# First block by token halves: output projection, queries and routing of tokens 0-127 ahead of the other half's attention

## The reference

```python
def first_block(...):
    ...
        h = rmsnorm(x, ln_mix_g[l]) * (1 + sc1) + sh1
        proj = h @ w_in[l]
        ...
        o_attn = nsa_mixer(q, kc, vc, ks, vs, kw, vw, gates, ...)
        o_conv = short_conv_mixer(ch, cb, cc, conv_w[l])
        mixed = jnp.concatenate([rmsnorm(o_attn, norm_attn_g[l]), rmsnorm(o_conv, norm_conv_g[l])], axis=-1)
        x = x + gt1 * (mixed @ w_out[l])

        h2 = rmsnorm(x, ln_ffn_g[l]) * (1 + sc2) + sh2
        x = x + gt2 * peer_ffn(h2, peer_wq[l], peer_keys[l], peer_u[l], peer_v[l])
    return rmsnorm(x, ln_final_g)
```

## Time and profile before

| | |
|---|---|
| median of 3 runs (lowest, highest) | 1507.47 us (1506.05, 1512.93) |
| profiled execution: its time, its span | 1513.2 us, 1511.3 us |
| mean granted TensorE clock | 0.948 of full |
| busy: PE, DVE, ACT, POOL | 1281.6 us (85%), 746.8 (49%), 477.1 (32%), 368.4 (24%) |
| gathers (q0 of the DMA queues) | 36864 packets, 268.45 MB, 43.3% of 16 engines' span |
| HBM read and written | 375.02 MB and 1.06 MB |

### The profile page before, as it was taken

How to read it: one execution, slowest core, us unless ns; L and a number is a source line. 1 busy time by engine, 2 the same in 40 slices (tenths; PEclk the granted TensorE clock), 3 DMA queues, 4 the chain that set the end, 5 groups by cost and what they waited for, 6 DMA issues and landing times.

```text
span 1511.3 us, 13142 instructions
## 1 busy us (share of the span) xinstructions
PE 1281.6 (85%) x4744; PEld 771.6 (51%) x4744; DVE 746.8 (49%) x1657; ACT 477.1 (32%) x1224; POOL 368.4 (24%) x285
## 2 busy tenths in 40 slices
PE   5899877887798887878889878699997789999896
PEld 1688545652233323223333322255775679999782
DVE  2313552748986696555544454511667764431212
ACT  1022220134343334344243333312785441111101
POOL 0688100134353454344334444100000000000000
PEclk9898888899999999999999999999998989999999
DMA  9775400599999999999999999645322130204130
GB/s 338 288 257 212 160 14 0 215 393 421 421 390 418 410 417 407 422 420 422 421 384 387 391 423 421 264 141 194 112 94 74 56 112 1 83 32 164 56 111 28
DMA packets 90827, 376.92 MB, mean 249 GB/s; under 512 B 6307, under 2 KB 8524, under 8 KB 57932
## 3 DMA queue, kind: packets, MB, share of 16 engines
q0 software_dynamic: 36864, 268.45, 43.3%
q1 hardware_dynamic: 52112, 103.46, 19.0%
q10 hardware_dynamic: 1788, 4.19, 0.9%
HBM read 375.02 MB, written 1.06 MB: 249 GB/s over the span
## 4 chain that ended last, share of the span: by engine, by line
PE 49%; DMA 21%; DVE 18%; ACT 8%; issue 2%; POOL 1%; SPq 0%; DVEq 0%; ACTq 0%; POOLq 0%
PE ps L87 49%; DMA AR<-in_puv,idx 19%; DVE AR L87 9%; DVE acc L87 3%; ACT L87 3%; DMA W<-in_w_mod 2%; ACT acc L87 2%; DVE tok L87 1%; ACT wv L87 1%; DVE RT L87 1%; ACT AR L87 1%; DVE hT L87 1%; ACT tok L87 1%; DVE junk L87 1%; POOL AR L87 1%
## 5 line engine op out<-in xcount | busy, mean ns | idle before, releaser
L87 PE MATMUL ps<-AR,acc 128*128 128x512 f32 x1024 | 500.5, 626 | 114.7 <-ACT acc L87 111.0
L87 DVE CUSTOM_DVE_ANT_0 AR<-AR,tok 128x1024 f32<-128x1024 f32 x256 | 312.6, 1223 | 219.0 <-DMA AR<-in_puv,idx 217.9
L87 POOL DMA_INDIRECT AR<-in_puv,idx x256 | 276.3, 1079 | 526.5 <-PE ps L87 390.3
L87 PEld LDWEIGHTS ps<-AR,acc 128*128 128x128 f32 x1024 | 183.8, 194 | 429.1 <-ACT acc L87 266.0
L87 PE MATMUL ps<-hT,W 128*128 128x256 f32 (+2 forms) x1504 | 323.1, 375 | 3.2 <-ACT hT L87 2.2
L87 PEld LDWEIGHTS ps<-hT,W 128*128 128x128 f32 (+1 forms) x1504 | 271.9, 198 | 46.1 <-issue 7.4
L87 ACT ACTIVATE wv<-av 128x1 f32<-128x1 f32 x256 | 51.5, 201 | 350.2 <-DVE av L87 349.9
L87 ACT ACT_TABLE_LOAD x90 | 115.5, 1283 | 16.8 <-issue 15.3
L87 ACT ACTIVATE acc<-K,wv 128x128 f32<-128x128 f32 x256 | 102.8, 402 | 8.4
L87 PE MATMUL ps<-W,hT 128*128 128x512 f32 (+3 forms) x288 | 95.2, 487 | 0.0
L87 ACT ACTIVATE wv<-wv,gw 128x1 f32<-128x1 f32 x256 | 75.4, 294 | 8.3
(11 more groups left out here) (199 smaller groups left out, 1035.8 us busy)
## 6 DMA issues: line engine op xcount, KB each, us to landing
W<-in_w_in SPq DMA_DIRECT2D x25, 2048.0 KB, 7.9
W<-in_w_mod SPq DMA_DIRECT2D x12, 2048.0 KB, 16.9
W<-in_w_out SPq DMA_DIRECT2D x2, 2048.0 KB, 10.3
W<-in_wq SPq DMA_DIRECT2D x2, 2048.0 KB, 10.3
AR<-in_puv,idx POOLq DMA_INDIRECT x256, 12.7
W<-in_wba SPq DMA_DIRECT2D x2, 2048.0 KB, 7.8
W<-in_wbb SPq DMA_DIRECT2D x2, 2048.0 KB, 7.7
W<-in_wo SPq DMA_DIRECT2D x2, 2048.0 KB, 7.8
```

The lines of the kernel that those rows point to most:

```text
L87: ins = f(*args, **kw)
```

## The change

The norms over the conv and attention channels, the convolution, the output projection's and the queries' functions take one half (and one weight tile) at a time. Emitted ahead of the gathers are half 0's parts, and of half 1's the units 4 and 5, `scores(6)` and the convolution. The rest of half 1 is a generator `half1`, which the loop over gathers advances by one piece per iteration from u = 1 on. The gathers begin with five slots (`ring`), since slots 5 and 6 lie over half 1's attention buffers in AR; these two are added when half 0's routing is done. `scores(u)` ends with the exponentials, and a new `weigh(u)` has its last three DVE operations, the normalisation. The routing has four batches of two heads (each pair of batches issues its `key_scores`), advanced by 2 DVE instructions per iteration below u = 32 and by 3 from there. Scratch moves: the keys into `R_LNF`, the routing's `sw` into `R_G2`, the scores of even units from 4 on into `R_POST`; so of the four broadcast rows only row 2 is loaded early and rows 1, 0 and 3 are loaded in the loop, and both halves of `mod_row` come together after half 1's routing. The diagonal matrices begin in the second half of `hT` and change to `acc[:, 0]` when `q_norm(1)` needs `hT`.

```diff
+        nrm = ar(4 * P).rearrange("p (n t) -> p n t", n=4)
+        junk = sb("junk", [P, D])
+        osq0 = junk[:, 0:512].rearrange("p (j t) -> p j t", j=4)
+        at[0] = 5 * 2 * D
...
-        for r in range(4):
-            SP.dma(nc.sync.dma_start, s_row, rowb[:, r, :], rows[r, :].partition_broadcast(P))
+        t_rows = {}
+
+        def load_row(r, after):
+            t_rows[r] = SP.dma(nc.sync.dma_start, s_rows[r], rowb[:, r, :], rows[r, :].partition_broadcast(P), after=after)
+
+        load_row(2, [])
...
+        def norm_root(key, n, src, after):
+            b = ps.take()
             for j in range(4):
-                t = V(stt, mixT[:, j, a * 128:a * 128 + 128], O[a].t[:, j * 128:j * 128 + 128], PV[:, V_NA + j:V_NA + j + 1],
-                      rat[:, a * 128:a * 128 + 128], MUL, MUL, after=[e, t_os[a]] + t_mc)
+                t = PE(mm, b.t[:, 0:P], ones, src[:, j, :], start=(j == 0), stop=(j == 3), after=b.old + after)
+            e = A(act, n, b.t[:, 0:P], ACT.Sqrt, scale=1.0 / 512, bias=eps, after=[t])
+            b.free = [e]
+            t_cn[key] = e
...
+        def attn_root(a):
+            t = A(act, osqs[a], O[a].t[:, :].rearrange("p (j t) -> p j t", j=4), ACT.Square,
+                  after=[stage[3 + 4 * a, "O"], stage[1 + 4 * a, "O"]] + t_g1 + t_c["o", 0] + t_c["o", 1])
+            t_os[a] = t
+            norm_root(("a", a), rats[a], osqs[a], [t])
+
+        def attn_mix(a):
+            e = V(rec, rats[a], rats[a], after=[t_cn["a", a]])
+            for j in range(4):
+                t = V(stt, mixT[:, j, a * P:a * P + P], O[a].t[:, j * P:j * P + P], PV[:, V_NA + j:V_NA + j + 1],
+                      rats[a], MUL, MUL, after=[e, t_os[a]] + t_mc)
+                t_mix[a].append(t)
             O[a].free = [t]
-            t_mix.append(t)
-        kT_sb = PT[:, 0, :]
+
+        t_oc, t_mix = [[], []], [[], []]
+        t_mc, t_g1 = [], []
+        kT_sb = R_LNF
         s_k = dsem("s_k")
-        t_keys = SP.dma(nc.sync.dma_start, s_k, kT_sb, keysT, after=[stage[7, "O"], stage[6, "O"]])
+        t_keys = SP.dma(nc.sync.dma_start, s_k, kT_sb, keysT)
...
-            for h0, nh in ((0, 2), (2, 2), (4, 4)):
-                bs, t = banks[h0 // 4]
+            for h0, nh in ((0, 2), (2, 2), (4, 2), (6, 2)):
+                if h0 % 4 == 0:
+                    bs, t = key_scores(a, h0 // 4)
...
-        ob1 = attn_mm(1)
-        routes = [route(0, kb, [stage[7, "O"]])]
+        qp = mixT
+        b2 = ps.take()
+        for n in range(4):
+            t_mc.append(mod_cols_sum(b2, 4 * n, *t_ms[n]))
+        sh2, sc2, t_m2 = mod_affine(b2, t_mc[3], 24, V_LNF, 16)
+        for n in range(2):
+            t_g1.append(mod_row_sum(2, n, *t_ms[4 + n]))
+        for j in range(4):
+            conv_step(j, 0)
+        turn_p(3)
+        pv_(2)
+        norm_root(("c", 0), nrm[:, 0, :], cbT[:, :, 0:P], t_oc[0])
+        pv_(3)
+        attn_root(0)
+        conv_mix(0)
+        scores(4)
+        attn_mix(0)
+        attn_mm(0, 0)
+        weigh(4)
+        for j in (0, 1):
+            conv_step(j, 1)
+        attn_mm(0, 1)
+        attn_add(0, 0)
+        turn_p(4)
+        scores(5)
+        attn_add(0, 1)
+        q_norm(0, [])
+        for j in (2, 3):
+            conv_step(j, 1)
+        weigh(5)
+        q_project(0, 0)
+        routes = [route(0, [])]
+        advance(routes[0], 1)
+        pv_(4)
+        turn_p(5)
+        norm_root(("c", 1), nrm[:, 1, :], cbT[:, :, P:2 * P], t_oc[1])
+        q_back(0)
+        q_project(0, 1)
+        scores(6)
         while (0, 0) not in t_idx or (0, 0) not in t_gw:
             advance(routes[0], 1)
-        attn_add(1, ob1)
-        queries(1)
-
+        pv_(5)
+        conv_mix(1)
+        ring = [[n, [t_gel[0], t_gel[1], t_cn["c", 1], t_mixfree[0]] + t_mix[1]] for n in range(5)]
+        late_t = {}
+
+        def half1():
+
+            weigh(6)
+            yield
+            turn_p(6)
+            load_row(1, [stage[6, "T"]])
+            yield
+            scores(7)
+            yield
+            pv_(6)
+            yield
+            weigh(7)
+            yield
+            turn_p(7)
+            yield
+            pv_(7)
+            yield
+            attn_root(1)
+            yield
+            attn_mix(1)
+            yield
+            attn_mm(1, 0)
+            yield
+            attn_mm(1, 1)
+            yield
+            attn_add(1, 0)
+            yield
+            attn_add(1, 1)
+            late_t["B"] = stage[7, "e"]
+            yield
+            late_t["dg"] = [t for f in dg_free for t in f]
+            q_norm(1, late_t["dg"])
+            yield
+            yield
+            q_project(1, 0)
+            yield
+            q_project(1, 1)
+            yield
+            q_back(1)
+            yield
...
-            slot_free[n] = [e]
+            ring.append([n, [e]])
             return e
 
         ahead = []
+        h1 = half1()
...
-            if routes:
-                advance(routes[0], 3)
-                if (0, 7) in t_gw and not second:
-                    second.append(1)
-                    routes = [route(1, [key_scores(1, 0), key_scores(1, 1)], [t_idx[0, 7], t_gw[0, 7]])]
-            if u in (64, 80):
-                t_g2.append(mod_row(3, (u - 64) // 16))
+            if u >= 1:
+                advance(h1, 1)
+            advance(routes[0], 2 if u < 32 else 3)
+            if (0, 7) in t_gw and len(routes) == 1 and len(t_h2[1]) == 2:
+                t_eq["hold"] = [late_t["B"]]
+                eqbuf[0] = acc[:, 1, :].rearrange("p (h s j) -> p h s j", h=4, s=16)
+                ring.append([5, [stage[7, "O"], t_mix[1][-1]]])
+                ring.append([6, [stage[7, "O"], t_mix[1][-1], t_eq["last"]]])
+                routes.insert(0, route(1, [t_idx[0, 7], t_gw[0, 7]]))
+            if (1, 7) in t_gw and len(routes) == 2:
+                routes.append(None)
+                load_row(0, [t_keyfree[-1]])
+                load_row(3, [t_idx[1, 7], t_gw[1, 7]])
+                for n in range(2):
+                    t_g2.append(mod_row(3, n))
```

More of the change, by code:

```diff
@@ L659, in build @@
-        t_mix = []
-        b = ps.take()
-        for j in range(4):
-            t = PE(mm, b.t[:, 0:S], ones, cbT[:, j, :], start=(j == 0), stop=(j == 3), after=b.old + [t_oc[j][1]])
-        rcv = z[:, 0, 0:S]
-        e = A(act, rcv, b.t[:, 0:S], ACT.Sqrt, scale=1.0 / 512, bias=eps, after=[t, t_oc[3][0]])
-        b.free = [e]
-        e = V(rec, rcv, rcv, after=[e])
-        for j in range(4):
-            t_mix.append(V(stt, mixT[:, 4 + j, :], oc[:, j, :], PV[:, V_NC + j:V_NC + j + 1], rcv, MUL, MUL, after=[e] + t_mc))
@@ L719, in queries @@
[L719 to L738 removed]
+        o_banks = {}
@@ new lines, in attn_mm, with attn_add @@
+        def attn_mm(a, n):
+            i, w, t_w = w_o[n]
+            b = ps.take()
+            t = token(w, 0, 512, mixT, a, t_w, t_mix[a], b, 0)
+            if a == 1:
+                done_w(i, t)
+            o_banks[a, n] = b, t
+            t_mixfree[a] = t
+        def attn_add(a, n):
+            b, t = o_banks[a, n]
+            o = junk[:, n * 512:n * 512 + 512]
+            xs = X[:, a, n * 512:n * 512 + 512]
+            e = V(tt_, o, b.t[:, :], R_G1[:, n * 512:n * 512 + 512], MUL, after=[t] + t_g1 + t_jx[-1:] + [t_cn["a", a]])
+            b.free = [e]
+            t_x1[a].append(V(tt_, xs, xs, o, ADD, after=[e]))
+            t_jx.append(t_x1[a][-1])
@@ new lines, in build, with q_norm, q_project @@
+        t_hx = {}
+        t_keyfree = []
+        def q_norm(a, free):
+            t_xb = norm_x(a, st[:, 12 + a:13 + a], t_x1[a], tok2, [stage[2 + 5 * a, "T"]])
+            t_hx[a], t_hx[a, "x"] = norm_T((a,), tok2, [t_xb], sc2, sh2, [t_m2] + free)
+        def q_project(a, n):
+            c = slice(a * 128, a * 128 + 128)
+            i, w, t_w = w_q[n]
+            b = ps.take()
+            for j in range(4):
+                for k in range(8):
+                    t = PE(mm, b.t[:, j * 128:j * 128 + 128], w[:, k, j * 128:j * 128 + 128], hT[:, k, c],
+                           start=(k == 0), stop=(k == 7), after=b.old + [t_w] + t_hx[a])
+            e = A(act, qp[:, 4 * n:4 * n + 4, c], b.t[:, :].rearrange("p (j t) -> p j t", j=4), ACT.Copy,
+                  after=[t, t_mixfree[a]])
+            b.free = [e]
+            t_qp[a].append(e)
+            if a == 1:
+                done_w(i, t)
@@ L1017, in build @@
                 rope("k", 0, t_rot["q", 0])
-        t_gfree = [f[0] for f in slot_free]
+        t_gfree = [f[0] for _, f in ring]
         t_pelast = e
```

179 lines of the change are left out of this document (68 added, 111 removed).

## The result

The changed kernel takes 1550.46 us (median of 4 runs, 1546.75 to 1558.36), the kernel before in the same session 1508.95 (4 runs, 1506.05 to 1512.93): ratio 1.028, 95% interval 1.0232 to 1.0328. It is slower by 41.5 us. The prediction had 1531 and a range to 1545: right in sign, too low in size, and the measured time lies above the range. The profiled execution has a span of 1549.8 us and a mean granted clock of 0.937 (before 1511.3 and 0.948).

What follows compares the result with a forecast made beforehand. The prediction took the DMA transfers of 256 expert-row gathers as the bound. Its terms, -9.3 + 3.7 + 24 + 3 - 1.5 + 3.7 = +23.6 us, moved the median from 1507.47 to 1531 us; range 1499 to 1545.

Steps and rivals of the forecast that it cites:

- First gather, 271: Start of the gathers: first gather at 271 us instead of 280.3, -9.3 us, bounds 263 and 278.
- scores(4) hold DVE to 194.0, the attention products end at 196.1: Steps ahead of the output projection: the attention root fits meanwhile, norm of the conv half ends at 189.7 us.
- The units, +24: Second half's pieces at units 1 to 19 among the gathers open transfer holes: +24 us, bounds 10 and 34.
- Only the lack of slots keeps them apart: Gathers with the second half: PE's 43 + 39 us of work against 85 us of transfers, separated by too few slots alone.
- +14: The units' idle if a gather takes 4.4 us by the Trainium skill, with an allowance of 3.5 us instead of 2.3.
- Five slots to unit 58, +3: Until head 7 is routed, comparisons and table loads exceed the 2.3 us allowance in three batches: +3 us (0 to 8).
- the dip, -1.5: Without long four-head comparisons in the routing, the transfer dip at 405 to 436 us goes: -1.5 us.
- mod_row, +3.7: Both mod_row calls together after route(1), near unit 121, hold up the dots: +3.7 us (0 to 9).
- Bytes, +3.7: Rows 0, 1 and 3 of rowb, 1.6 MB, move into the gathers' stretch at 422 GB/s: +3.7 us.
- Rival 1: Faster: the second half hides among units 1 to 58, the start counts alone; 1500.4 us, or 1492; 12%.
- Rival 3: Worse: idle among the units at 34 us, DVE's queue carrying dot, routing and softmax; 1541 or 1548 us; 15% above 1538.
- Rival 2: No difference within 0.5%: start at 263 to 267 and idle of 10 to 19 us together, about 1507 us; 18%.

Runs made afterwards that it cites:

- the kernel with small pieces: Changed kernel with scores(6) later, half 1 cut into small pieces, mod_row at units 64 and 80: 1519.64 us with slots 5 and 6 early, 1518.86 with five slots.
- the best: Changed kernel with small pieces, scores(6) later, slots 5 and 6 early, mod_row at 64 and 80, both key_scores at route(1)'s start: 1512.85 us, ratio 1.0018.
- the kernel with the attention's block: Changed kernel, half 1's remaining attention as one block behind five gathers' issue, then seven slots, small pieces; scores(6) later, mod_row at 64 and 80: 1518.0 us.

## Why the prediction was low

By its own terms, against the parts above (their sum is 42.8 at the last gather, the prediction's 23.6):

- **First gather, 271: mis-sized by 5.5 us.** It came at 276.5, and at 276.5 to 280.8 in seven executions with this start (mean 278.3), against 278.3 to 280.3 in four of the old start (mean 279.5). Of the 9.3 us some 1 to 4 exist. What failed are the steps up to "scores(4) hold DVE to 194.0, the attention products end at 196.1", 6.9 us in all: row sums 1.5, convolution and norm 0.9 to 1.0 each (a half step takes 1.6 us, not 1.4), and scores(4) 3.5, since on PE they stood behind the root that was said to fit meanwhile and ran at the lower clock (1.8 of the 3.5), and DVE waited for them. From the queries on the step count held: 45.2 us from there to the first gather, 46.7 predicted (whose 236.8 is 0.7 above its own summands; PE waited 0.7 there in the trace, for ACT's copy).
- **The units, +24: mis-sized by 7.0 us**, the largest miss. The mechanism is right: POOL gaps near 10 us at the fourth gather after the start and behind the projections, share 0.79 for the first 117 us (0.7 was forecast for 110). By share alone the idle is 25 us, against 1 before, the 24 of the sum. What the sum left out is that the transfers move less while they count as busy: 34.1 MB in 0.79 x 117.3 = 92.7 us are 368 GB/s, in place of 418 (422 / 1.01); that they are draining then is how I read it, and no run tests it. And a queries unit lasts 10.7 us, not 8.7. The bounds (10 to 34) held it. By the Trainium skill ("DMA: Bandwidth & Descriptors", the anatomy of one DMA) the term would have been +14; the first gather's dot started 5.6 us after its issue (276.50 to 282.10) and 31 us were lost, so the trace speaks against it.
- **The reason given for it is only half right.** "Only the lack of slots keeps them apart" predicts that slots help; two slots some 45 units earlier gave 2.5 us with coarse pieces (8 in the trace's stretch) and nothing that the times show with small ones (6 in the trace). Size and order of pieces gave 14 and 9 us. What the runs leave open is why such different arrangements (a block or pieces, five or seven slots) end on the same time, and what PE's lower clock costs in the first units (0.87 on average there, 0.92 before).
- **Five slots to unit 58, +3, and the dip, -1.5: together 3.4 where 1.5 was predicted.** The +3 is borne out: five slots lost 4.0 us more than seven between the 25th and 60th gather in the kernel before and 4.2 in the kernel with small pieces. The -1.5 isn't: the smaller batches gave nothing.
- **mod_row, +3.7: 6.3 us more than before were lost from the 60th to the 140th gather, but only 2.2 us at the pair.** Moving it back gave nothing. The second key_scores inside the routing took 4.4 us of trace time, although the ring had seven slots: an exponential with its table loads, a combine and the scores follow one another, and DVE holds four dots meanwhile. No term of the sum had it.
- **Bytes, +3.7: 5.2 up to the last issue**, of which 1.6 MB are the rows. The load of rows costs its bytes.
- **Rival 1 (it hides, 12%)** had PE's sum equal to the transfers'. It isn't reached by any arrangement tried: the best starts 18.6 us sooner and has 19.5 us more between first and last gather. **Rival 3** (1541 to 1548) came nearest, with its bound of 34 us, but its cause, the routing steps in DVE's queue, isn't shown.
- **Rival 2 (no difference)**: a start at 263 to 267, idle of 10 to 19 us, the rows' 3.7 and the other terms' 5.2 add up to 1509 to 1522, so its "about 1507" is at or below the low end of its own terms. The measured time is far from either.

No version of the new order beat the kernel before; the best of them, 1512.85 us, is 0.2% slower.

## What to carry to other kernels

When a stretch is bound by transfers, work that stands ahead of it costs its own length once, and the same work placed at its beginning can cost more than twice that: moving 11 us of it cost 25. A likely reason, not tested by itself, is that each piece delays the release of buffers through every in-order queue it touches. Sum such losses in bytes over the full rate, not in idle share, and not by the time of one gather either, since other transfers can have moved across it (33 us at the 25th gather were 16 us of loss). And before pricing a piece, look for each place where one engine waits for another with the bulk work queued behind it; one wait of 6 us that no sum had was worth about as much as two slots of the ring.

## What was unexpected of the hardware

- DMA share and rate part where the share falls: 368 GB/s per busy time over the first 117 us of the changed kernel, 339 (105 / 0.31) in the emptiest window of the kernel with the attention's block, 398 (394 / 0.99) in the first 81 us of the kernel before, 418 (422 / 1.01) in the full stretch.
- PE's clock was granted 1.2 GHz again by the first combine after 5.61 us of idle, although 20.87 us of matmuls at 2.4 GHz stood ahead (0.43 us per record and a granted clock of 1.00 there; then 3.75 us for four records, which take 1.98 at full clock, at a granted clock of 0.50).
